# A woven projection unit of the gated DeltaNet inverse, cut in two halves around a small product

## The reference, cut to what matters

```python
proj = h @ w_in
qkv, z, b_raw, a_raw, qd, kd, vd = jnp.split(proj, CD_SPLITS, axis=-1)
...
m = jnp.where(strict, jnp.einsum('nbhcd,nbhsd->nbhcs', kb, k) * decay, 0.0)
rhs = jnp.concatenate([v * beta[..., None], kb * jnp.exp(gc)[..., None]], axis=-1)
sol = lax.linalg.triangular_solve(m + jnp.eye(c, dtype=F32), rhs, left_side=True, lower=True)
...
o = _rms(o) * norm_w.astype(F32) * jax.nn.silu(z.astype(F32).reshape(hd))
```

## Time and profile before

| | |
|---|---|
| median of the runs (3) | 1221.82 us (1220.36 to 1222.19) |
| profiled execution, its own time | 1221.61 us |
| its span, first to last instruction | 1219.8 us |
| mean granted TensorE clock | 0.969 of full speed |
| PE busy | 1118.9 us, 92% of the span |
| DVE busy | 883.1 us, 72% |
| ACT busy | 628.0 us, 51% |
| PE's share of the chain that ended last | 67% |

### The profile page before, as it was taken

How to read it: one execution, slowest core, us unless ns; L and a number is a source line. 1 busy time by engine, 2 the same in 40 slices (tenths; PEclk the granted TensorE clock), 3 DMA queues, 4 the chain that set the end, 5 groups by cost and what they waited for, 6 DMA issues and landing times.

```text
span 1219.8 us, 28160 instructions
## 1 busy us (share of the span) xinstructions
PE 1118.9 (92%) x10185; PEld 1076.2 (88%) x10185; DVE 883.1 (72%) x1909; ACT 628.0 (51%) x1317; POOL 21.0 (2%) x12
## 2 busy tenths in 40 slices
PE   5999999989999999999999997589987999999996
PEld 5899988979889999989999985589876988999996
DVE  3587745759878888987887674875644887888854
ACT  1376455344466665445666536066523436666542
POOL 0000000000000000000000001200100000000000
PEclk9799899999999999999999998789999999999998
DMA  9457525527836656943775521012202673666661
GB/s 362 152 159 243 184 83 177 190 67 300 285 97 185 182 180 200 361 146 97 233 224 171 191 70 35 2 50 82 82 1 84 208 262 87 181 180 186 177 199 59
DMA packets 54831, 195.60 MB, mean 160 GB/s; under 512 B 6067, under 2 KB 8115, under 8 KB 54492
## 3 DMA queue, kind: packets, MB, share of 16 engines
q1 hardware_dynamic: 54748, 194.45, 48.9%
HBM read 193.36 MB, written 1.07 MB: 159 GB/s over the span
## 4 chain that ended last, share of the span: by engine, by line
PE 67%; DVE 7%; ACT 2%; issue 1%; DVEq 0%; ACTq 0%
PE proj L507 41%; PE acc L507 25%; DVE yr L1483 1%; DVE off_bd L1691 1%; DVE state L1765 1%; DVE yr L1506 0%; DVE h_lo L1479 0%; PE acc L696 0%; DVE sys_t L1699 0%; DVE o_tok L1792 0%; DVE k_tok L1681 0%; DVE conv L1712 0%; DVE w_lo L1359 0%; ACT w_hi L1017 0%; DVE ada_sum L1373 0%
## 5 line engine op out<-in xcount | busy, mean ns | idle before, releaser
L1017 ACT ACTIVATE w_hi<-raw 128x512 fp32r<-128x512 f32 x528 | 328.7, 625 | 174.5 <-PE acc L507 127.4
L1359 DVE TENSOR_TENSOR w_lo<-raw,w_hi 128x512 fp32r<-128x512 f32 x528 | 358.5, 684 | 79.0 <-ACT w_hi L1017 77.8
L507 PE MATMUL proj<-h_hi,w_hi 128*128 128x256 f32 x1352 | 386.5, 286 | 3.9 <-DVE h_lo L1479 3.2
L507 PE MATMUL proj<-h_lo,w_hi 128*128 128x256 f32 x1352 | 383.2, 283 | 0.0
L507 PE MATMUL proj<-h_hi,w_lo 128*128 128x256 f32 x1352 | 383.1, 283 | 0.0
L507 PEld LDWEIGHTS proj<-h_hi,w_hi 128*128 128x128 f32 x1352 | 259.1, 192 | 8.4 <-issue 3.6
L507 PEld LDWEIGHTS proj<-h_lo,w_hi 128*128 128x128 f32 x1352 | 259.1, 192 | 0.0
L507 PEld LDWEIGHTS proj<-h_hi,w_lo 128*128 128x128 f32 x1352 | 259.0, 192 | 0.0
L507 PE MATMUL acc<-a_hi,w_hi 128*128 128x256 f32 (+1 forms) x608 | 172.4, 284 | 3.6 <-DVE a_lo L1646 2.0
L507 PE MATMUL acc<-a_lo,w_hi 128*128 128x256 f32 (+1 forms) x608 | 170.6, 281 | 0.0
L507 PE MATMUL acc<-a_hi,w_lo 128*128 128x256 f32 (+1 forms) x608 | 170.2, 280 | 0.0
(11 more groups left out here) (261 smaller groups left out, 1578.5 us busy)
## 6 DMA issues: line engine op xcount, KB each, us to landing
raw<-in_w_stream SPq DMA_DIRECT2D x264, 512.0 KB, 3.6
ada_long<-in_ada_stream SPq DMA_DIRECT2D x52, 512.0 KB, 6.6
ada_first<-in_ada_stream SPq DMA_DIRECT2D x20, 512.0 KB, 4.6
ada_ssd<-in_ada_stream SPq DMA_DIRECT2D x12, 512.0 KB, 4.4
ada_out<-in_ada_stream SPq DMA_DIRECT2D x12, 512.0 KB, 5.7
hankel<-bias_scratch SPq DMA_DIRECT2D x2, 1024.0 KB, 5.9
x<-in_x_tiles SPq DMA_DIRECT2D x1, 1024.0 KB, 10.1
out_tiles<-x SPq DMA_DIRECT2D x1, 1024.0 KB, 3.9
```

The costliest lines, as they stand in the source:

```text
L507: return pe.matmul(out, a, b, start=start, stop=stop, skip_group_check=True)
L1017: act.activation(hi, src, ACT.Copy).then_inc(w_rounded, 1)
L1359: dve.tensor_tensor(lo, src, hi.bitcast(F32), ALU.subtract).then_inc(w_split, 1)
```

## The change

Each of the twelve woven z units is no longer given in one piece of 24 matmuls before S(m). Its first half (blocks 0 to 3, 12 matmuls) stands before S(m), and its second half (blocks 4 to 7, 12 matmuls) stands between S(m) and T(m). The wait for the bank is made before the first half only, and the wait for the split weights before each half, as before. The matmuls are the same in number, operands and accumulation order. Nothing is changed on any other engine.

```diff
+            def project_half(name, k, a):
+
+                n = PARTS[name][0] + k
+                if a == 0 and before[n] is not None:
+                    s, at, _ = freed[before[n]]
+                    pe.wait_ge(s, at)
+                pe.wait_ge(w_split, 2 * n + a + 1)
+                hi, lo, _ = w_half(n, a)
+                for q in range(4):
+                    t = 4 * a + q
+                    for p_, (u, v) in enumerate(((hi, h_hi), (hi, h_lo), (lo, h_hi))):
+                        last = mm(banks[n][:, 0:SEQ], u[:, q], v[:, t], t == 0 and p_ == 0, t == 7 and p_ == 2)
+                last.then_inc(w_used, 1)
...
                         if at <= ZT:
-                            project("z1", some=(at - 1,))
+                            project_half("z1", at - 1, 0)
                         if lv < LEVELS - 1:
                             pe.wait_ge(i_y, at)
                             pe.wait_ge(i_bd, at)
                             stacks(BANKS[3 + m], it_bd, sy, m).then_inc(i_z_mm, 1)
+                        if at <= ZT:
+                            project_half("z1", at - 1, 1)
                         pe.wait_ge(i_y_bd, at)
                         stacks(BANKS[m], sy_bd, it, m).then_inc(i_zt_mm, 1)
```

## The result

The changed kernel is slower, and by more than was forecast. Over 13 runs of each its median is 1230.01 us (1223.15 to 1234.46), that of the kernel before 1222.36 us (1217.56 to 1227.74). The ratio of the two, worked out over all these runs, is 1.0055, with a 95% interval of 1.0036 to 1.0075; it stands for 6.7 us, where the medians lie 7.7 apart. Two later comparisons, each on a chip of its own, gave 1.0066 (1.0044 to 1.0089) and 1.0055 (1.0034 to 1.0076). The forecast of 1225.7 had the sign right, but its range ended at 1227.8.

The account below looks back on a forecast made before the run. The prediction took TensorE, busy 92% of the span, as the bound. Switches 3.1, table-load stall 0.84 and level starts 0 gave +3.9 us on 1221.61, 1225.5, named as 1225.7 with the median's 0.2; range 1222.6 to 1227.8.

Parts of the forecast that it names:

- Where TensorE stands: Levels 1 to 4 of the inverse: TensorE busy 18.00 of 18.00 us per level, so nothing to win.
- The switches: Levels 1 to 4: one more change between z and small matmuls and back per unit, 12 x 0.26 = 3.1 us.
- T to the next unit takes 1.03, 0.05 more: Return from T(m) to the next z unit: 1.03 us against 0.98 from S to T, 0.05 extra.
- Switches hidden: Levels 1 to 4: added switches cost nothing, only stalls of +0.8 to +1.0 remain, 1222.7 us; chance 0.17.
- second reading: Switch price from a whole unit's period: 5.09 us less 2.87 and 1.93 for its matmuls leaves 0.29.
- The table load: Level 1: the first silu, behind a 1.28 us table load, holds up the next z unit; one 0.84 us stall.
- S(0) at the level starts, T, the weights, the loads: Starts of levels 2 to 4: slack of 2.4 us gone, stall taken as 0; no wait at the others.
- The sum of the stretch: First z unit to T of level 5: 3.1 plus 0.84 plus 0, +3.9 us, from 72.1 to 76.0.
- Nothing behind the inverse gives it back: After the inverse: the scan waits for T of level 5, so none of the +3.9 us is recovered.
- a stage outside the stretch that changes by more than a microsecond: Sign of a wrong prediction: a length change over a microsecond outside first z unit to T of level 5.
- ScalarE becomes the bound: Levels 1 to 4: ScalarE late, 0.2 at 8 hand-overs and 0.3 at 3 level starts, 1228.2 us; chance 0.08.
- Faster: Before the scan: TensorE's 1.28 us idle hangs on GpSimd clearing `resid`, earlier S shortens it, 1220.5 us; chance 0.04.

Follow-up runs that it names:

- merged: Against the kernel before: z in two PSUM banks, whole units 0 and 1 ahead of S(0), unit 2 ahead of S(2) in each level; ratio 0.9977.
- mid64: Whole z units as before the change, plus one unread small matmul with 64 output rows mid-unit; first z unit to scan's first matmul 81.88 us.
- mid128: Whole z units as before the change, plus one unread small matmul with 128 output rows mid-unit; first z unit to scan's first matmul 79.16 us.
- two_banks: Changed kernel with the z units in two PSUM banks in turn; ratio 1.0036.
- preload: Changed kernel with one unread one-column silu added on ScalarE ahead of level 1; first z unit to scan's first matmul 80.52 us.
- thirds: Against the changed kernel: z units in pieces of 3, 3 and 2 blocks, S(m) in two halves between; first z unit to scan's first matmul 86.70 us.

## Why the prediction was wrong

**Where TensorE stands.** Right. The stretch had nothing to win, and the changed kernel won nothing there.

**The switches.** The mechanism was right, the size too small. Forecast 12 x 0.26 = 3.1 us, measured 12 x (5.42 - 5.09) = 4.0. The failing term is "T to the next unit takes 1.03, 0.05 more". It took S to T (0.98) as a block without a switch, and used the same row against the rival *Switches hidden*, but S itself comes from z, and 0.98 holds the entry into the small products. A block between its own kind takes 0.94 (`merged`). The 0.05 should have been 2 x 1.08 - 2.01 = 0.15. With it the sum is 0.09 + 0.15 + 0.12 = 0.36 per unit, against 0.33 measured; the 0.24 read at the first z unit is 0.23 at the others, which takes off 0.01, and what is left is of the size to which starts are given. The prediction's second reading, 0.29 from the whole period, had the same fault in smaller measure: its 0.030 per small matmul was taken over a block of 96 with its return. The two readings agreed because they shared it. Which rule this supports is also sharper now. The row at 128*64 against 128*128 in the scan and the 0.23 between `mid64` and `mid128` both speak for the rule on a change of tiling mode in the Trainium skill, TensorEngine Tiling (Array Packing), Key Properties. The other half of the price does not follow from that rule.

**The table load.** Right in place, cause and almost in size: forecast 0.84, measured 0.80 (1.88 - 1.08), and gone by `two_banks` and by `preload`.

**S(0) at the level starts, T, the weights, the loads.** Right: no wait in the changed kernel, 0 was taken. The slack was indeed all but used up, to 0.07 us, and `thirds` shows the wait that comes with any more.

**The sum of the stretch.** 3.9 forecast, 4.8 measured (81.33 - 76.54).

**Behind the inverse.** The sentence "Nothing behind the inverse gives it back" was true, but the prediction stopped there and took the rest as unchanged. It looked at the clock only for whether the new idle moment lowers it, which it doesn't: in levels 2 to 4 it stays 1.00. The term for the rest stood at nothing without a reason, and this is the second step that failed, the one that put the time outside the range: with the stretch alone set right the sum would be 1221.8 + 4.8 = 1226.6, inside 1222.6 to 1227.8. The prediction's own sign for it, a stage outside the stretch that changes by more than a microsecond, came true. What it left out is that TensorE's clock steps down at the scan's end for some microseconds already (0.83 in the window there, in the kernel before), and that lengthening the stretch by 4.8 us changes how much of the output projection falls under it, through the time since the clock's last rise. That costs 341.46 - 339.95 = 1.5 us in the profiles of this length, padded ones included. That it costs as much in the timed runs is not shown by them.

Both together make 4.8 + 1.5 = 6.3 us, or 0.52%, inside each of the three measured intervals (1.0055, 1.0066, 1.0055). The single ratios lie 0.4 to 1.8 us above it. Whether more than chance is in that stays open.

Of the rivals, *Switches hidden* is refuted by the period of 5.42, *ScalarE becomes the bound* by the single wait in the stretch and by `preload`, although its 1228.2 was nearer to the result than the forecast, which is luck and no merit of its mechanism, and *Faster* by the unchanged idle time of 1.28 us ahead of the scan.

## What to carry to other kernels

Where TensorE is full, weaving two sorts of matmuls costs at each return, here 0.33 us between wide 128*128 and narrow 128*64 ones. Weave in the largest pieces that the waits of the other engines allow, and read the price of a block from one that stands between its own kind, not from one at an edge. A delay of a few microseconds can cost more or less than its length, because the stages behind it meet the clock's low moments elsewhere (here what follows changed by -0.2 to +1.5 us over the kernels tried): padding a kernel to the same length with plain work tells this from the change's own cost.

## What the runs showed of the hardware

One unread matmul of 64 output rows in the middle of a z unit costs 0.45 us, no less than a block of sixteen with its semaphore waits (0.33 beside the matmuls' own time); the same with 128 output rows costs 0.22. Sixteen small matmuls take 0.94 us between their own kind and 1.08 alone between z matmuls. Lengthening one stage by 2.6 us left what lies behind at 340.0 us, by 4.8 us made it 341.5 and by 5.4 us 340.8, with the granted clock at 0.83, 0.66 and 0.83 from 56 to 76 us behind the scan's first matmul, and at 1.00, 0.97 and 0.97 from 76 to 140. The silu's table load took 1.28 us and waited for TensorE together with its silu; one silu of one column, placed earlier, took 0.8 us off TensorE's path.
